# Units dealt out between the column sums of a gap and behind its first tiles, two low parts first, tiles that serve two weight units

## The reference

```python
def rmsnorm(x, g):
    xf = x.astype(jnp.float32)
    xf = xf * lax.rsqrt(jnp.mean(xf * xf, axis=-1, keepdims=True) + EPS)
    return (xf * g.astype(jnp.float32)).astype(x.dtype)

def modulate(x, g, shift, scale):
    return rmsnorm(x, g) * (1 + scale) + shift

def swiglu(h, wg, wu, wd):
    return (jax.nn.silu(h @ wg) * (h @ wu)) @ wd
...
def trunk_layer(x, cond, p, l, ctx, rows, cols):
    mod = jax.nn.silu(cond) @ p['ada_w'][l] + p['ada_b'][l]
    m = jnp.split(mod[:, None, :], 9, axis=-1)
    h = modulate(x, p['norm_pre'][l, 0], m[0], m[1])
    y = swiglu(h, p['ffn_gate'][l, 0], p['ffn_up'][l, 0], p['ffn_down'][l, 0])
    x = x + 0.5 * m[2] * rmsnorm(y, p['norm_post'][l, 0])
    h = modulate(x, p['norm_pre'][l, 1], m[3], m[4])
    y, new_ctx = token_mixer(h, p, l, ctx, rows, cols)
    x = x + m[5] * rmsnorm(y, p['norm_post'][l, 1])
    h = modulate(x, p['norm_pre'][l, 2], m[6], m[7])
    y = swiglu(h, p['ffn_gate'][l, 1], p['ffn_up'][l, 1], p['ffn_down'][l, 1])
    x = x + 0.5 * m[8] * rmsnorm(y, p['norm_post'][l, 2])
    return x, new_ctx
```

## Time and profile before

| what | value |
|---|---|
| median of 3 runs | 2199.2 us (2198.91 to 2199.8) |
| the profiled execution's own time | 2199.55 us |
| its span, first to last instruction | 2197.8 us |
| PE busy | 2142.3 us, 97% of the span, mean granted clock 0.983 |
| DVE, ACT, POOL busy | 892.9, 930.4, 1233.3 us (41%, 42%, 56%) |
| share of PE in the chain that ended last | 78% |
| mean HBM traffic | 141 GB/s |
| L603, three products per weight tile, on h | 537.9 + 535.6 + 535.5 us |

### The profile page before, as it was taken

How to read it: one execution, slowest core, us unless ns; L and a number is a source line. 1 busy time by engine, 2 the same in 40 slices (tenths; PEclk the granted TensorE clock), 3 DMA queues, 4 the chain that set the end, 5 groups by cost and what they waited for, 6 DMA issues and landing times.

```text
span 2197.8 us, 33516 instructions
## 1 busy us (share of the span) xinstructions
PE 2142.3 (97%) x13737; PEld 2048.6 (93%) x13737; DVE 892.9 (41%) x1572; ACT 930.4 (42%) x1389; POOL 1233.3 (56%) x972
## 2 busy tenths in 40 slices
PE   7999999999899999999999999999998999999998
PEld 7999998988899999999989999899888999899998
DVE  4221126446766454222251221445576564621111
ACT  4222333345766543223333233324567646423232
POOL 2766553434478454666646666453444965376663
PEclk9999999999999999999999999999999999899998
DMA  8555674433223374445554437553232245244432
GB/s 291 179 155 181 231 247 145 127 86 90 68 87 105 115 280 125 132 138 175 182 180 134 144 120 239 185 154 92 79 88 77 87 125 174 67 143 126 127 118 72
DMA packets 313073, 311.46 MB, mean 142 GB/s; under 512 B 9924, under 2 KB 293848, under 8 KB 312920
## 3 DMA queue, kind: packets, MB, share of 16 engines
q1 hardware_dynamic: 305815, 303.55, 44.4%
q10 hardware_dynamic: 7104, 5.77, 0.8%
HBM read 305.35 MB, written 3.93 MB: 141 GB/s over the span
## 4 chain that ended last, share of the span: by engine, by line
PE 78%; DVE 8%; ACT 6%; POOL 4%; issue 2%; SPq 1%; DMA 1%; DVEq 0%; ACTq 0%
PE X L603 55%; PE S L603 9%; PE Ab L603 5%; POOL w_lo L543 2%; PE S L639 1%; PE Ab L639 1%; PE X L732 1%; ACT w_hi L1097 1%; POOL dec L571 1%; POOL dec L570 1%; PE X L840 1%; PE S L869 1%; ACT p L1296 1%; PE X L922 1%; SPq L521 1%
## 5 line engine op out<-in xcount | busy, mean ns | idle before, releaser
L543 POOL TENSOR_TENSOR w_lo<-raw,w_hi 128x512 fp32r<-128x512 f32 (+1 forms) x872 | 1156.0, 1349 | 931.1 <-ACT w_hi L1097 922.1
L1097 ACT ACTIVATE w_hi<-raw 128x1024 fp32r<-128x1024 f32 (+1 forms) x436 | 453.3, 1042 | 652.8 <-PE X L603 621.0
L603 PE MATMUL X<-h_hi,w_hi 128*128 128x384 f32 x1600 | 537.9, 336 | 4.4 <-DVE h_lo L1662 3.5
L603 PE MATMUL X<-h_lo,w_hi 128*128 128x384 f32 x1600 | 535.6, 335 | 0.0
L603 PE MATMUL X<-h_hi,w_lo 128*128 128x384 f32 x1600 | 535.5, 335 | 0.0
L603 PEld LDWEIGHTS X<-h_hi,w_hi 128*128 128x128 f32 x1600 | 301.2, 188 | 11.9 <-issue 5.9
L603 PEld LDWEIGHTS X<-h_lo,w_hi 128*128 128x128 f32 x1600 | 301.2, 188 | 0.0
L603 PEld LDWEIGHTS X<-h_hi,w_lo 128*128 128x128 f32 x1600 | 301.2, 188 | 0.0
L1730 DVE TENSOR_TENSOR prod<-X,silu 128x768 f32<-128x768 f32 x44 | 42.1, 958 | 549.7 <-PE X L603 549.7
L603 PE MATMUL X<-act_hi,w_hi 128*128 128x384 f32 x704 | 235.7, 335 | 0.0
L603 PE MATMUL X<-act_hi,w_lo 128*128 128x384 f32 x704 | 235.2, 334 | 0.0
(11 more groups left out here) (404 smaller groups left out, 3135.7 us busy)
## 6 DMA issues: line engine op xcount, KB each, us to landing
raw<-in_w_in SPq DMA_DIRECT2D x124, 512.0 KB, 3.8
raw<-in_ffn_gate SPq DMA_DIRECT2D x88, 512.0 KB, 3.8
raw<-in_ffn_up SPq DMA_DIRECT2D x88, 512.0 KB, 3.8
raw<-in_ffn_down SPq DMA_DIRECT2D x80, 512.0 KB, 3.5
raw<-in_ada_w SPq DMA_DIRECT2D x48, 512.0 KB, 3.6
hold<-in_ada_w SPq DMA_DIRECT2D x29, 512.0 KB, 6.4
first_w<-in_ada_w SPq DMA_DIRECT2D x16, 512.0 KB, 8.8
hold_a<-in_ada_w SPq DMA_DIRECT2D x16, 512.0 KB, 8.3
```

The lines of the kernel that those rows point to most:

```text
L543: ins = nc.gpsimd.tensor_tensor(slot(w_lo, u)[:, part], raw_of(u)[:, part], slot(w_hi, u)[:, part], SUB)
L603: mm = nc.tensor.matmul(dst, w[:, k, m * 128:m * 128 + 128], r_, start=start and k + j == 0, stop=stop and k == u.nk - 1 and j == 2)
L1097: A(slot(w_hi, u), raw_of(u), ACT.Copy).then_inc(hi_ready[u.split], 1)
```

## The change

**Units.** `y_sums` runs unit 2 between its two sets of sums. Units 3, 4, 5 and 6 go one at a time between the following sets of sums. Behind `cross_ready` come units 7 to 10 instead of 3 to 6, behind the second spread units 11 to 15 instead of 7 to 21, and units 16 to 21 go in pairs behind tiles 1, 2 and 3 of `by_tiles`. In the gap with 8 units, unit 7 alone stands behind `cross_ready`, and nothing behind the second spread.

**Tiles.** In `by_tiles` each of the eight tiles serves two w units: tiles 4 to 7 multiply `head[2]` and `head[3]` one after the other, as tiles 0 to 3 do with `head[0]` and `head[1]`.

**VectorE.** `add_to_x(1)` moves ahead of the wait for `cross_ready`; tile 2's addition takes the place of tile 1's around the second root. Behind the second spread `low(0)` and `low(1)` follow `sq` of tile 1 at once, ahead of `ada_take` and of all additions; `low(2)` follows `sq` of tile 3. The wait for VectorE's own `sq` now stands directly behind it.

```diff
--- before.py
+++ after.py
@@ -690,7 +690,7 @@
                             mm.then_inc(S["half_done"], 1)
                     mm.then_inc(unit_done[u.split], 1)
 
-            def by_tiles(head):
+            def by_tiles(head, riders=()):
 
                 def part(u, k):
                     if k % 4 == 0:
@@ -712,15 +712,13 @@
                             part(head[k // 4 * 2], k)
                             part(head[k // 4 * 2 + 1], k)
                     return
-                for k in range(4):
+                for k in range(KT):
                     pe.wait_ge(S["h_ready"], seen.next("h_ready"))
-                    part(head[0], k)
-                    part(head[1], k)
-                for k in range(4, KT):
-                    pe.wait_ge(S["h_ready"], seen.next("h_ready"))
-                    part(head[2], k)
-                for k in range(4, KT):
-                    part(head[3], k)
+                    part(head[k // 4 * 2], k)
+                    part(head[k // 4 * 2 + 1], k)
+                    if k:
+                        for u in riders[2 * k - 2:2 * k]:
+                            ada_unit(u)
 
             def tokens(rows):
 
@@ -739,11 +737,13 @@
                     mm = nc.tensor.transpose(dst[:, b * 128:b * 128 + 128], col[:, b:b + 1].broadcast_to([128, 128]), ident)
                 mm.then_inc(S["spread_ready"], 1)
 
-            def y_sums():
+            def y_sums(between=()):
 
                 pe.wait_ge(S["y_sq_ready"], seen.next("y_sq_ready", KT))
                 pe.wait_ge(S["y_added"], seen.next("y_added", 6))
                 token_sums(S5, prod[:, 0, :], True, False)
+                for u in between:
+                    ada_unit(u)
                 pe.wait_ge(S["parts_ready"], seen.next("parts_ready"))
                 token_sums(S5, silu[:, 0, :], False, True).then_inc(S["sum_ready"], 1)
 
@@ -751,26 +751,29 @@
 
                 for u in units[:2]:
                     ada_unit(u)
-                y_sums()
+                y_sums(units[2:3])
+                ada_unit(units[3])
                 pe.wait_ge(x_free[0], seen.value(("xf", 0)) + 1)
                 token_sums(X[0][:, 0, 0:NB], y_sum, True, False)
-                ada_unit(units[2])
+                ada_unit(units[4])
 
                 pe.wait_ge(S["r_ready"], seen.next("r_ready"))
                 spread(SPREAD[0], r_t)
                 token_sums(X[0][:, 1, 0:NB], silu[:, 1, :], True, False)
+                ada_unit(units[5])
                 pe.wait_ge(S["parts_ready"], seen.next("parts_ready"))
                 token_sums(X[0][:, 0, 0:NB], part, False, True)
+                ada_unit(units[6])
                 pe.wait_ge(S["c_made"], seen.next("c_made", KT))
                 token_sums(X[0][:, 1, 0:NB], prod[:, 1, :], False, True).then_inc(S["cross_ready"], 1)
-                for u in units[3:7]:
+                for u in units[7:11]:
                     ada_unit(u)
 
                 pe.wait_ge(S["r_ready"], seen.next("r_ready"))
                 spread(SPREAD[1], r_t)
-                for u in units[7:]:
+                for u in units[11:2 * KT]:
                     ada_unit(u)
-                return by_tiles
+                return lambda head: by_tiles(head, units[2 * KT:])
 
             def x_sums():
 
@@ -1681,6 +1684,7 @@
                 inverse_root()
                 dve.wait_ge(S["spread_ready"], seen.next("spread_ready"))
                 add_to_x(0)
+                add_to_x(1)
 
                 dve.wait_ge(S["cross_ready"], seen.next("cross_ready"))
                 step(V.tensor_tensor(grown[:, :], X[0][:, 1, 0:NB], r_t[:, :], MUL))
@@ -1689,10 +1693,9 @@
 
                 step(V.scalar_tensor_tensor(grown[:, :], x_sum[:, :], -1.0, grown[:, :], MUL, ALU.max))
                 V.tensor_tensor(x_sum[:, :], x_sum[:, :], grown[:, :], ADD).then_inc(S["x_sum_made"], 1)
-                step(V.tensor_tensor(y[:, 1, :], y[:, 1, :], SPREAD[0], MUL))
+                step(V.tensor_tensor(y[:, 2, :], y[:, 2, :], SPREAD[0], MUL))
                 inverse_root()
-                step(V.tensor_tensor(x[:, 1, :], x[:, 1, :], y[:, 1, :], ADD))
-                add_to_x(2)
+                step(V.tensor_tensor(x[:, 2, :], x[:, 2, :], y[:, 2, :], ADD))
                 dve.wait_ge(S["spread_ready"], seen.next("spread_ready"))
 
                 dve.wait_ge(S["ada_used"], units[2].n + 1)
@@ -1700,13 +1703,15 @@
                     for g, (t0, t1) in GROUPS:
                         ins = V.scalar_tensor_tensor(sq[:, k, t0:t1], x[:, k, t0:t1], mA[:, k, g:g + 1], SPREAD[1][:, t0:t1], MUL, MUL)
                     ins.then_inc(S["norm_ready"], 1)
+                    dve.wait_ge(S["norm_ready"], seen.next("my_norm"))
                     if k == 1:
-                        ada_take(units[7])
-                    if k:
+                        low(0)
+                        low(1)
+                        ada_take(units[KT - 1])
+                    if k > 2:
                         low(k - 1)
-                    if k + 3 < KT:
-                        add_to_x(k + 3)
-                    dve.wait_ge(S["norm_ready"], seen.next("my_norm"))
+                    if k and k + 2 < KT:
+                        add_to_x(k + 2)
                 low(KT - 1)
 
             def last_post():
```

## The result

The changed kernel is slower. The prediction said 2190.7 us and had left 0.06 for slower. The runs lie further apart than usual, and this has to be known to read them: TensorE's clock falls at other moments in each, and the mean granted clock of the changed kernel goes from 0.977 in the run of 2220.4 us to 0.986 in that of 2201.2. The profiled execution is one of the better ones, 2205.34 us, with a span of 2203.5.

The account below looks back on a forecast made before the run. TensorE was taken as the bound, at half rate for some 58 us, nearly all in the gaps. Gains of 2.2, two at 3.1, -1.4 and 1.5 made 8.5 us: 2199.2 to 2190.7, range 2184.5 to 2200.5.

Parts of the forecast that it names:

- The step on the clock: In the gaps, units dealt between sums were taken to hold the full clock, three of four 22-unit gaps keeping it.
- The price of a fall: 22-unit gap, clock falling after the second set of sums: 1.1 to 2.3 us lost, less 0.3 won; -1.4 us.
- second rival: Clock falls as often as today; units 7 to 10 outlast the root; 2201 with one gap kept, at worst 2206; chance 0.08.
- the 0.3 won behind it: Behind the first `sq` after the second spread: TensorE ends at 22.8 us instead of 23.1, worth 0.3 us.
- The gain of a kept clock: 22-unit gap at full rate: first `sq` 3.1 us earlier, gap 3.2 us shorter in sum, 3.1 used.
- The prices of units, sets and pairs: TensorE in the gaps: unit 0.43 us full rate, 0.84 half; set of sums 0.74 full, 1.21 half.
- 1.1 us of idle: Behind the second spread: TensorE idle 1.1 us ahead of tile 2, waiting for VectorE.
- VectorE binds: Rival: clock holds, but low parts 2 to 5 come 1 us later each; 2192 to 2194 us; chance 0.12.
- 0.85 for layer 0: Gap0 of layer 0: `proj` copy waits for VectorE, whose work grows by eight waits, 0.85 us; gain 2.2 instead of 3.1.
- The 8-unit gap: `sq` 2.9 us earlier, first tile 1.5 sooner behind it; 4 at best, -1 at worst, 1.5 us gain taken.
- some 2.5 us: 8-unit gap: TensorE still idles some 2.5 us ahead of tile 0, where the clock fell before.
- the signs of being wrong: Half rate for 10 us in four gaps or more; idle over 2 us at tiles 2 to 5; `w_lo` wait behind tile 7.

Follow-up runs that it names:

- late products alone: Kernel before plus three unread full-array products at each of six places from the second set of sums on, 18 a gap: 2214.68 us, ratio 1.0071.

## Why the prediction was wrong

Two steps failed, of like weight. The forecast counted on half-rate time that did not go away (80 us in the mean after, 77 before), and it had no price for the turns, and too low a one for the waits, that the new order makes. The profiled execution tells the two apart. It lost 5.8 us where 8.5 were to be won, a miss of 14.3. At the forecast's own prices, with the falls that came (one 22-unit gap at 3.1, three at -1.4, the short gap at 1.5), it would have won 0.4: so 8.1 of the miss are the clock, and 6.2 the prices.

**The step on the clock.** The prediction took "the side of it holding", because units had brought the clock back. It named the alternation as denser than the stretch that lost the clock and thinner than the one that won it back, and chose between them by how close together the units stand. The runs show two mistakes in that. What weighs most is the early stretch, in which the change put one lone unit, and one lone unit there is not enough (the kernel with 21 products and this unit fell in some gaps, and no longer with three products beside it). And behind a fall the dealt units did not bring the clock back: in the changed kernel the last set starts 12.2 us into gap1 of layer 0 and the clock rises 17.4 us into it; in the gap between the layers before, 9.2 and 13.6 (1121.2 - 1107.59); in the same gap of the kernel with one dealt unit, where 6.8 us are at half rate, 7.8 and 11.9. In all the 22-unit gaps of the kernels without unread products, a fall that began ahead of the last set ended 4.0 to 7.3 us behind the start of that set, while units stood in a row with at most the second spread among them. The dealt units moved that set 3 us back.

The forecast had three 22-unit gaps of four with the clock up; the profiled execution had one, at a clock of 0.985 where the mean of the 15 runs is 0.982.

**The price of a fall was mis-sized.** "-1.4" was -1.7 and -2.8 where the half rate lasted 10.2 us and -3.8 where it lasted 13.7. The mechanism was the one named in the second rival, units 7 to 10 at half rate ahead of the second spread: VectorE's wait for it grew from 0.44 to 1.91 us. The sizes were not. The prediction's times, 1123.5 to 1124.7, put the first `sq` 1.4 to 2.6 us later than before; it wrote "1.1 to 2.3 lost", which has the 0.3 won behind it taken off already, and took it off once more. In gap1 of layer 0 the `sq` came 3.4 later, since a set behind a unit and a lone unit are dearer at half rate too, and behind it 0.4 was lost and not 0.3 won (23.6 us from the first `sq` to the end of the measure against 23.2). That is why the second rival ended at 2206 at worst, and gave 2201 for one kept gap, the case of the profiled execution, which took 2205.3.

**The gain of a kept clock was right in kind.** In the gap that kept it, the first `sq` came 2.8 us sooner (3.1 forecast) and the gap was 2.4 us shorter (3.2). What is missing is in the prices below.

**The prices of units, sets and pairs were taken from rows of their like.** 0.43 came from eight units in a row; a lone one is 0.57 at full and 1.01 at half rate (0.84 forecast). 1.21 for a set came from three in a row; between two units it is 1.37. A pair was priced at 0.86 and is 1.21 behind a tile. Four more lone units 0.56, the sets some 0.25, three pairs 1.05, and the waits ahead of tiles 0 and 2 (0.35 + 0.47), less 0.57 saved at the second set, make 2.1 us a gap. That sum is worked out from rows; the kernels with the clock held measured 2.3 to 2.9. The prediction's own sum behind the second spread had 1.1 us of idle and no turn in it, and gave 0.3 us won behind the first `sq`, where 0.4 was lost.

**VectorE was read rightly.** The low parts of tiles 0 and 1 were forecast at 2.5 and 3.3 behind the first `sq`:

```profile
1124.97 1.51 DVE L1704 SCALAR_TENSOR_TENSOR sq<-x,mA,S 128x128 f32<-128x128 f32 x4
1126.71 1.41 DVE L1665 SCALAR_TENSOR_TENSOR h_lo<-sq,mB,h_hi 128x128 fp32r<-128x128 f32 x4 [0.22 <-ACT h_hi L1189]
```

The first tile's ends at 1127.45, 2.5 behind, the second's at 1128.1, 3.1 behind. Idle ahead of tile 2 was 0.47 and not 1.1, because TensorE had waited 0.35 ahead of tile 0 and the pair took longer. The rival "VectorE binds" did not happen in the 22-unit gaps. `proj` made TensorE wait 0.43 us in gap0 of layer 0 and 0.17 in that of layer 1, where before it was 0.88 and nothing, and where the prediction had added 0.85 for layer 0. The smaller wait there is luck, as far as the trace tells: from the last low part to the copy VectorE's small operations took 4.5 us instead of 5.7, and one of them, the last `lbl`, took 0.16 instead of 1.34 us with no edit to it. It took either time in other kernels here, and why is open.

**The 8-unit gap** was to gain 1.5 and gained 0.65 (37.45 against 38.10 us by the same measure), with 13.7 instead of 17 us of it at half rate. Its first `sq` was to come 2.9 us earlier and came 0.2 earlier, 14.6 behind the gap's first unit instead of 14.8; the first tile came 1.4 sooner behind it, as forecast. The forecast's idle of "some 2.5 us" ahead of tile 0 is there, and so are three more waits and the one for `w_lo` that stood among the signs of being wrong: GpSimd writes the next unit's low part until 1929, and TensorE's products resume at 1929.06 instead of 1928.84.

```profile
1908.73 0.69 PE L603 MATMUL X<-h_hi,w_hi 128*128 128x384 f32 x1 [2.64 <-DVE h_lo L1665]
...
1917.26 0.45 PE L603 MATMUL X<-h_hi,w_hi 128*128 128x384 f32 x1 [0.25 <-DVE h_lo L1665]
1919.87 0.45 PE L603 MATMUL X<-h_hi,w_hi 128*128 128x384 f32 x1 [0.25 <-DVE h_lo L1665]
1922.49 0.44 PE L603 MATMUL X<-h_hi,w_hi 128*128 128x384 f32 x1 [0.23 <-DVE h_lo L1665]
```

**What stays open.** Why one fall lasts 3.4, 6.8, 10.2 or 13.7 us in gaps of the same kernel is not settled; the runs show which edits move the shares. What the Trainium skill, TensorE: Matmul & The Clock Gate, Part 4, says of transposes, which the prediction weighed for the spread, no run here tries.

## What to carry to other kernels

Fill a wait with independent work where the wait is: one unit in a 0.86 us wait won 7 us, and the whole change, with that unit, four more among operations that did not wait, and the edits around them, lost 14. Take the price of an operation from a row in which its neighbours are those it will have, since each turn between kinds of work on TensorE cost 0.14 to 0.35 us here. Where a kernel lives at the edge of the clock, look first at what the engine did ahead of each fall and only then at the sparse stretch after it, compare the time times the mean clock as well as the time, and trust no single run.

## What the runs showed of the hardware

- TensorE's clock can be down while the engine is busy without a pause. In the kernel with late products alone it was 13.60 us busy of 13.60 at half rate, among them 18 full-array products. The Trainium skill, TensorE: Matmul & The Clock Gate, Part 1, ties the half rate to stretches in which the engine is idle; here the idle 0.9 us lay ahead of the fall, and nothing idle kept it down.
- The moment and the number of the falls differ from run to run of one kernel. The Trainium skill, TensorE: Matmul & The Clock Gate, Part 1, says of a kernel's start that the number of cold matmuls differs between runs of one kernel. The runs here show the like in the middle of a kernel: 0.977 to 0.986 of mean clock in 15 runs, 19 us apart.
- Work that computes nothing can pay: 12 full-array products a gap, 1.3 us, made the kernel 12.4 us faster.
- A turn between 384-column products on the full array and units on 32-column tiles costs 0.35 us there and back, with no wait in the trace. Between sums a unit is 0.14 dearer than in a row (0.57 against 0.43), and between units a set of 3-column sums is 0.18 dearer than between 256-column products (0.76 against 0.58).
